# Finishing each expert's rows in the expert loop instead of in a combine stage (one decoder layer, one core)

## The reference

```python
# xt: 512 x 1024; 4 groups of 8 experts; each token picks 1 group and 2 experts in it
weights = g_w[:, None] * softmax(top_v)              # two weights per token
expert  = g_idx[:, None] * EXPERTS_PER_GROUP + top_i # two experts per token
h = silu(xb @ w_e_gate[e]) * (xb @ w_e_up[e])        # 1024 -> 512, twice
y = h @ w_e_down[e]                                  # 512 -> 1024
moe = sum of the token's two y rows, each times its weight
out = LayerNorm(ALPHA * x2 + moe)                    # ln2_g, ln2_b
```

## Time and profile before

| | us |
|---|---|
| median of 3 runs (lowest, highest) | 1359.92 (1359.82, 1360.22) |
| the profiled execution | 1359.31 |
| its span, first to last instruction | 1357.6 |
| TensorE busy in the span | 1235.4 (91%) |
| VectorE busy | 509.0 (37%) |
| ScalarE busy | 411.0 (30%) |
| GpSimd busy | 118.6 (9%) |
| mean granted TensorE clock | 0.969 |

### The profile page before, as it was taken

The page is one execution under the profiler, slowest core; times in us unless marked ns, Lnnn a source line. Parts: engine busy times, 40 slices in busy tenths (PEclk is TensorE's granted clock), DMA queues, the critical chain, the costliest instruction groups (busy, mean ns, idle before and its releaser), DMA issues.

```text
span 1357.6 us, 16490 instructions
## 1 busy us (share of the span) xinstructions
PE 1235.4 (91%) x5912; PEld 837.5 (62%) x5912; DVE 509.0 (37%) x780; ACT 411.0 (30%) x572; POOL 118.6 (9%) x168
## 2 busy tenths in 40 slices
PE   7999999999999999999998967999998888888860
PEld 6888878878888888888887863444433333333320
DVE  5487655336473473474348342000000000000008
ACT  5767673222432432432434021111111111111111
POOL 0000000000000000000051000211111111111112
PEclk9999999999999999999999976999999999999995
DMA  7232322353223133233233868999999999999954
GB/s 238 80 111 58 87 70 82 118 150 95 76 78 109 62 93 93 62 97 89 64 107 121 314 250 318 400 404 406 406 404 407 409 407 408 397 406 397 404 224 167
DMA packets 202069, 294.15 MB, mean 217 GB/s; under 512 B 11678, under 2 KB 109070, under 8 KB 201520
## 3 DMA queue, kind: packets, MB, share of 16 engines
q1 hardware_dynamic: 195568, 281.00, 57.7%
q0 software_dynamic: 5312, 8.47, 1.7%
q10 hardware_dynamic: 1152, 4.19, 0.8%
HBM read 289.89 MB, written 12.65 MB: 223 GB/s over the span
## 4 chain that ended last, share of the span: by engine, by line
PE 71%; DMA 19%; DVE 4%; SPq 3%; issue 2%; ACT 1%; POOLq 0%; ACTq 0%; POOL 0%; DVEq 0%
PE bank L1384 18%; PE bank L1385 18%; PE bank L1386 18%; DMA m_raw<-in_w_e_down_dram 9%; DMA m_raw<-in_w_e_up_dram 9%; PE bank L1624 8%; PE bank L1646 4%; SPq L388 2%; PE bank L1634 2%; PE bank L1558 1%; PE bank L1607 1%; DVE x L1372 1%; DVE wo_lo L881 1%; PE bank L1486 1%; DMA xg<-x_dram,first_x 0%
## 5 line engine op out<-in xcount | busy, mean ns | idle before, releaser
L1624 PE MATMUL bank<-m_raw,xe 128*64 128x512 f32 x1024 | 243.3, 610 | 34.4 <-DMA m_raw<-in_w_e_up_dram 29.3
L1384 PE MATMUL bank<-xt_hi,w_hi 128*128 128x512 f32 x576 | 225.0, 391 | 2.2 <-ACT merge L684 1.0
L1386 PE MATMUL bank<-xt_hi,w_lo 128*128 128x512 f32 x576 | 224.2, 389 | 0.0
L1385 PE MATMUL bank<-xt_lo,w_hi 128*128 128x512 f32 x576 | 224.1, 389 | 0.0
L881 DVE TENSOR_TENSOR w_lo<-raw,w_hi 128x1024 fp32r<-128x1024 f32 x120 | 148.4, 1238 | 184.7 <-ACT w_hi L595 183.3
L1624 PEld LDWEIGHTS bank<-m_raw,xe 128*64 128x64 f32 x1024 | 67.8, 138 | 184.0 <-issue 118.6
L595 ACT ACTIVATE w_hi<-raw 128x1024 fp32r<-128x1024 f32 x120 | 126.1, 1056 | 172.2 <-PE bank L1386 172.1
L1646 PE MATMUL bank<-m_raw,ht 128*64 128x512 f32 x512 | 121.3, 601 | 10.3 <-DMA m_raw<-in_w_e_down_dram 8.7
L1384 PEld LDWEIGHTS bank<-xt_hi,w_hi 128*128 128x128 f32 x576 | 108.1, 188 | 25.6 <-ACT merge L684 1.4
L1386 PEld LDWEIGHTS bank<-xt_hi,w_lo 128*128 128x128 f32 x576 | 108.1, 188 | 22.3
L1385 PEld LDWEIGHTS bank<-xt_lo,w_hi 128*128 128x128 f32 x576 | 108.2, 188 | 22.2
(11 more groups left out here) (237 smaller groups left out, 1630.7 us busy)
## 6 DMA issues: line engine op xcount, KB each, us to landing
m_raw<-in_w_e_gate_dram SPq DMA_DIRECT2D x64, 1024.0 KB, 16.0
m_raw<-in_w_e_up_dram SPq DMA_DIRECT2D x64, 1024.0 KB, 14.9
m_raw<-in_w_e_down_dram SPq DMA_DIRECT2D x64, 1024.0 KB, 14.0
raw<-in_w_in_dram SPq DMA_DIRECT2D x88, 512.0 KB, 4.0
raw<-in_w_ret_o_dram SPq DMA_DIRECT2D x16, 512.0 KB, 3.4
raw<-in_w_lru_o_dram SPq DMA_DIRECT2D x16, 384.0 KB, 3.0
raw<-in_w_out_dram SPq DMA_DIRECT2D x8, 512.0 KB, 3.5
y_rows<-y_dram SPq DMA_DIRECT2D x4, 1024.0 KB, 7.9
```

Of the source, the lines that this page charges most:

```text
L1384: pe.matmul(dst, sh, mh, start=first and x == 0, stop=False)
L1385: pe.matmul(dst, sh, ml, start=False, stop=False)
L1386: ins = pe.matmul(dst, sl, mh, start=False, stop=last and x == n - 1)
L1624: last = pe.matmul(bank[side:side + ROWS, b, :], xe[:, 4 * half + k, :], m_raw[v.slot][:, FE * k:FE * k + FE], start=half == 0 and k < 2, ...
```

## The change

- Rows are handled in halves of 512 columns: partitions 0 to 63 hold the left half of up to 64 rows, 64 to 127 the right half. `xg` becomes three buffers of 128x512, `turn_x` four 128x128 transposes.
- A token's pick with the lower expert number is its first, the other its last. `y_out` multiplies by the pick's weight. The first pick's row is scattered to `y_dram` (zeroed early in the kernel, so that it holds zeros where nothing came first); the last pick's expert gathers it (`y_first`), adds ALPHA times x2 (`base`) and its own y (`total_row`), takes statistics, lets TensorE join the two halves' means and variances (`moments`), normalises (`finish`) and scatters the rows to the output.
- The combine stage and the scaling of x2 by ALPHA on ScalarE go.
- The ring has 21 buffers, filled by a list ORDER, in which the last expert's gate comes before and its up after the down of expert 30; nine units instead of seven are loaded before the projection is done.
- The experts are written out instead of looped.
- The router also builds lists of the picks that are first and last and of their weights (32 more small matmuls and about 15 small VectorE operations).

```diff
-MRING = 18
+ORDER = [(part, 0, half) for part in "gu" for half in range(2)]
+for _e in range(EXPERTS - 2):
+    ORDER += [(part, _e + (part != "d"), half) for part in "gud" for half in range(2)]
+ORDER += [(part, _e, half) for part, _e in (("g", EXPERTS - 1), ("d", EXPERTS - 2), ("u", EXPERTS - 1), ("d", EXPERTS - 1)) for half in range(2)]
+AT = {what: n for n, what in enumerate(ORDER)}
+M_END = len(ORDER)
+MRING = 21
...
+            def load_m(slot, consumed, part, e, half):
+                sp.wait_ge(m_done, consumed)
+                w, k, n = {"g": (w_gate, 4, FE), "u": (w_up, 4, FE), "d": (w_down, 2, D)}[part]
+                src = w[:, e, k * half:k * half + k, :] if isinstance(e, int) else w[:, ds(e, 1), k * half:k * half + k, :].rearrange("p e k n -> p (e k) n")
+                sp.dma_start(m_raw[slot][:, :].rearrange("p (k n) -> p k n", k=k), src).then_inc(m_loaded[slot], 16)
+
+            def load_units(a, b):
+                for n in range(a, b):
+                    load_m(n % MRING, n + 1, *ORDER[n])
+
+            load_units(0, 9)
             sp.wait_ge(proj_ok, TT)
+            load_units(9, 16)
+            for side_h in range(2):
+                for x, name in enumerate(("ln2_g", "ln2_b")):
+                    sp.dma_start(ln2[ROWS * side_h:ROWS * side_h + ROWS, x, :],
+                                 io[name][0:1, HALF * side_h:HALF * side_h + HALF].rearrange("a n -> (a n)").partition_broadcast(ROWS)).then_inc(ln2_in, 16)
             sp.wait_ge(x2_ok, TT)
+            load_units(16, 17)
             sp.wait_ge(routed, TT)
+            load_units(17, 18)
+            sp.wait_ge(x2_stored, 16 * TT)
+            sp.wait_ge(x2_turned, TT)
+            load_units(18, 20)
+            sp.wait_ge(picks_ok, 1)
+            load_units(20, M_END)
...
+            pool.memset(zeros[:, :], 0.0).then_inc(list_set, 1)
+            pool.wait_ge(list_set, 3)
+            pool.wait_ge(conv_ok, 3)
+            pool.dma_start(y_dram.rearrange("(n p) d -> p n d", p=P), zeros[:, :].unsqueeze(1).to_broadcast([P, 2 * TOKENS // P, HALF])).then_inc(y_empty, 16)
...
-            def rows_next(e, first_turn=None):
-                pool.wait_ge(xe_turned, e + 3)
-                pool.sem_inc(marks, 1)
-                gather(e + 3, first_x)
-                if first_turn is None:
-                    free_y(e - 1)
-                else:
-                    with pool.If(first_turn > 0):
-                        free_y(e - 1)
-                send(e, e, first_y)
-
-            with pool.Fori(0, TURNS) as i:
-                steps.enter(i, 2 * BODY)
-                for b in range(BODY):
-                    rows_next(BODY * i + b, None if b else i)
-                steps.leave(TURNS)
-            rows_next(EXPERTS - 2)
-            free_y(EXPERTS - 2)
-            send(EXPERTS - 1, EXPERTS - 1, first_y)
-            free_y(EXPERTS - 1)
+            for e in range(3):
+                rows_in(xg[:, e, :], x2_halves, col(all_x, e), xg_in[e])
+            pool.wait_ge(picks_read, 3)
+            for e in range(EXPERTS):
+                if 3 <= e + 2 < EXPERTS and e > 0:
+                    pool.wait_ge(z0_ok, e)
+                    pool.wait_ge(xe_turned, e)
+                    rows_in(xg[:, (e + 2) % 3, :], x2_halves, col(all_x, e + 2), xg_in[(e + 2) % 3])
+                pool.wait_ge(y_ok, e + 1)
+                rows_out(y_dram, y_sb[:, :], col(all_first, e), y_sent)
+                if e + 1 < EXPERTS:
+                    pool.wait_ge(z0_ok, e + 1)
+                    pool.wait_ge(y_sent, 16 * e + 16)
+                    rows_in(y_first[:, :], y_dram, col(all_last, e + 1), y_first_in)
+                pool.wait_ge(f_ok, e + 1)
+                rows_out(out_halves, z[:, e % 2, :], col(all_last, e), stored[e % 2])
...
+            def y_out(s, consumed, w):
+                act.wait_ge(m_done, consumed)
+                if not (isinstance(s, int) and s == 0):
+                    act.wait_ge(y_sent, 16 * s)
+                    act.wait_ge(z_done, s + (isinstance(s, int) and s == EXPERTS - 1))
+                act.activation(y_sb[:, :], bank[:, 2, :], ACT.Identity, scale=w).then_inc(y_ok, 1)
+
+            def root(s):
+                act.wait_ge(f_var, s + 1)
+                act.activation(std[:, :], lnv[:, 3:4], ACT.Sqrt, bias=eps[:, :]).then_inc(f_std, 1)
...
+            act.wait_ge(ovf_ready, 1)
+            gate_evict(used("g", 0))
             xe_out(1)
             silu_part(0)
+            act.wait_ge(picks_read, 3)
+            for e in range(EXPERTS - 1):
+                gate_evict(used("g", e + 1))
+                if e:
+                    root(e - 1)
+                if e + 2 < EXPERTS:
+                    xe_out(e + 2)
+                y_out(e, used("d", e), all_w[:, e:e + 1])
                 silu_part(e + 1)
+            root(EXPERTS - 2)
+            y_out(EXPERTS - 1, used("d", EXPERTS - 1), all_w[:, EXPERTS - 1:EXPERTS])
+            root(EXPERTS - 1)
...
+            def h_part(s, hb):
                 dve.wait_ge(m_silu, s + 1)
+                tt(ht[:, hb, :, :], bank_t[:, 1, :, :], silu[:, :, :], ALU.mult).then_inc(ht_ok, 1)
+            def base(s, xb, zb, landed, free):
+                dve.wait_ge(xg_in[xb], landed)
+                if not (isinstance(s, int) and s == 0):
+                    dve.wait_ge(y_first_in, 16 * s)
+                if not (isinstance(s, int) and s < 2):
+                    dve.wait_ge(stored[zb], free)
+                dve.scalar_tensor_tensor(z[:, zb, :], xg[:, xb, :], ALPHA, y_first[:, :], ALU.mult, ALU.add).then_inc(z0_ok, 1)
+            def total_row(s, zb):
+                dve.wait_ge(z0_ok, s + 1)
+                if isinstance(s, int) and s == EXPERTS - 1:
+                    dve.wait_ge(m_done, used("d", s))
+                    dve.scalar_tensor_tensor(z[:, zb, :], bank[:, 2, :], all_w[:, s:s + 1], z[:, zb, :], ALU.mult, ALU.add).then_inc(z_done, 1)
+                else:
+                    dve.wait_ge(y_ok, s + 1)
+                    tt(z[:, zb, :], z[:, zb, :], y_sb[:, :], ALU.add).then_inc(z_done, 1)
+                dve.wait_ge(z_done, s + 1)
+                step(dve.bn_stats(stats[:, 0:6], z[:, zb, :]))
+                step.wait()
+                dve.sem_inc(marks, 1)
+                dve.bn_aggr(pairs[:, :], stats[:, 0:6]).then_inc(pairs_ok, 1)
+            def finish(s, zb):
+                zt = z[:, zb, :]
+                dve.wait_ge(paired, s + 1)
+                step(dve.tensor_copy(lnv[:, 0:3], bank[:, 6, 0:3]))
+                step.wait()
+                dve.scalar_tensor_tensor(lnv[:, 3:4], lnv[:, 2:3], lnv[:, 2:3], lnv[:, 1:2], ALU.mult, ALU.add).then_inc(f_var, 1)
+                step(dve.scalar_tensor_tensor(zt, zt, lnv[:, 0:1], ln2[:, 0, :], ALU.subtract, ALU.mult))
+                dve.wait_ge(f_std, s + 1)
+                step(dve.reciprocal(rstd[:, :], std[:, :]))
+                step.wait()
+                dve.scalar_tensor_tensor(zt, zt, rstd[:, :], ln2[:, 1, :], ALU.mult, ALU.add).then_inc(f_ok, 1)
+            def used(part, e):
+                return AT[part, e, 1] + 1 + MRING
+            up_evict(used("u", 0))
+            h_part(0, 0)
+            dve.wait_ge(picks_read, 3)
+            dve.wait_ge(ln2_in, 64)
+            for e in range(EXPERTS - 1):
+                late = e == EXPERTS - 2
+                if not late:
+                    up_evict(used("u", e + 1))
+                if e:
+                    finish(e - 1, (e - 1) % 2)
+                base(e, e % 3, e % 2, 16 * (e // 3 + 1), 16 * (e // 2))
+                total_row(e, e % 2)
+                if late:
+                    up_evict(used("u", e + 1))
+                h_part(e + 1, (e + 1) % 2)
+            e = EXPERTS - 1
+            finish(e - 1, (e - 1) % 2)
+            base(e, e % 3, e % 2, 16 * (e // 3 + 1), 16 * (e // 2))
+            total_row(e, e % 2)
+            finish(e, e % 2)
...
+            def turn_x(s, xb, landed):
+                pe.wait_ge(xg_in[xb], landed)
                 if not (isinstance(s, int) and s == 0):
                     pe.wait_ge(xe_ok, s)
                 pe.sem_inc(marks, 1)
+                for j in range(KD // 2):
+                    last = pe.transpose(bank_x[:, j, :], xg[:, xb, P * j:P * j + P], ident[:, :])
                 last.then_inc(xe_turned, 1)
...
+            def moments(s):
+                pe.wait_ge(pairs_ok, s + 1)
+                if not (isinstance(s, int) and s == 0):
+                    pe.wait_ge(f_var, s)
+                pe.matmul(bank[:, 6, 0:2], mean_of[:, :], pairs[:, :], start=True, stop=True)
+                pe.matmul(bank[:, 6, 2:3], diff_of[:, :], pairs[:, 0:1], start=True, stop=True).then_inc(paired, 1)
+            turn_x(0, 0, 16)
+            gate_up(0, 0)
+            turn_x(1, 1, 16)
             pe.wait_ge(ovf_ok, 1)
             pe.transpose(bank[0:1, 7, 256:256 + P], ovf_col[:, :], ident[:, :]).then_inc(ovf_turned, 1)
-            pe.wait_ge(fold_ok, 2)
```

(74 more changed lines are left out.)

385 lines of the change are left out of this document (160 added, 225 removed).

## The result

The change makes the kernel slower by a fifth: 1628.3 us (1624.2 to 1632.2, four runs) against 1359.9; the ratio is 1.198, with a 95% interval of 1.196 to 1.201. The forecast was 1620, range 1525 to 1715. The profiled execution took 1632.2 for a span of 1630.4. Of the runs behind this page, two of the kernel before and one each of the two experiments with eight dummies and with 18 ring buffers fell into a slower state, and all medians leave them out.

The account below looks back on a forecast made before the run. The prediction took the weight stream to bound the kernel before, and a serial gather the changed one: 856.5 + 29 x 25.3 + 28 = 1618 us of span, plus 2.3, gives 1620 us; range 1525 to 1715.

Parts of the forecast that it names:

- The main step: GpSimd's queue: gather of rows e+2 waits behind finish(e-1) and the output scatter, in series with TensorE; stall 9.3 us per expert.
- GpSimd: wake, scatter, gap: Between finish and gather: 0.79 from releasing event, 1.04 scatter, 0.8 before the second indirect DMA; sum 2.6 us.
- gather, issue to landing: Indirect DMA of rows e+2 into xg: 4.0 us, between 2.4 alone and 6.0 under a saturated weight stream.
- clock: TensorE after each stall: granted clock falls, costing 3.0 us extra per expert, ends 0 and 3.6.
- period: One expert of the serial loop: 13.0 work, 9.3 stall and 3.0 clock make 25.3 us, against the stream's 15.6.
- it runs dry near the time at which the gather's data start: Weight stream refilling six units: 15.6 us of transfers; the gather's data start 15.2 us after down.
- Rival (a): Gather meets a still backed-up weight stream and takes 6.0 us; period 27.3, time 1678; chance 0.20.
- The fit of the Trainium skill: GpSimd DMA as 2.0 us plus bytes over 436 GB/s: 2.3 us per mean gather, final figure about 50 us lower.
- Start and tail: Before the serial loop: 2.0 us later start, gate/up at 856.5; after fold(30): 28 us to the end.
- What was set down as hidden: Work off the critical path, costing nothing: table loads, y chain (14.3 us after a down), zero fill, h_part.
- Rival (b): TensorE's clock stays up or falls only briefly in the stall; period 22.3, time about 1531; chance 0.20.
- (c): Expert loop: chain fits under the weight stream, period 15.6 us, tail gains 35; time 1324; chance 0.05.

Follow-up runs that it names:

- eight dummies: Changed kernel with eight unused float32 matmuls on TensorE between moments and the transposes, inside the stall; 1594.0 us.
- 18 ring buffers: The kernel with the gather issued ahead of the f_ok wait, its ring cut from 21 to 18 weight buffers; 1328.9 us, ratio 0.979.
- half the traffic: Changed kernel with every weight load after the first 21 cut to its first half, instructions and waits kept; 1574.6 us, ratio 1.160.
- ten dummies: Changed kernel with ten unused matmuls on TensorE between moments and the transposes, inside the stall; 1569.7 us.
- e1_early: Changed kernel with only the gather moved: rows e+3 requested right after the scatter of y(e), no longer behind f_ok; 1322.0 us, ratio 0.974.
- e1_again: e1_early run once more unchanged, beside the run with two dummies for the last expert; 1319.9 us, ratio 0.974.

## Why the prediction was right

The main step, that the order of GpSimd's queue puts the gather of rows e+2 in series with TensorE in 29 iterations, is shown by the chain of waits and by the run that moves only that issue (1628 to 1322). It was found by following one iteration through the queues in program order, at a place where the trace of before shows no wait.

Term by term, forecast against measured:

| term, us per expert | forecast | measured |
|---|---|---|
| up eviction with wake | 0.74 | 0.71 |
| finish | 1.9 | 1.86 |
| GpSimd: wake, scatter, gap | 0.79 + 1.04 + 0.8 | 0.83 + 1.01 + 0.30 |
| gather, issue to landing | 4.0 | 5.34 |
| wake of TensorE | 0.1 | 0.14 |
| clock | 3.0 | 2.25 |
| gate, up, down, fold, transposes at full clock | 13.0 | 13.1 |
| period | 25.3 | 25.67 |

The measured terms add up to 25.55; of the missing 0.12, 0.09 is a single period in which the output scatter started 2.5 us late.

Three terms were off and nearly cancelled: over 29 periods the gather was taken 39 us too low, the gap and the clock together 36 us too high. That the mechanism was right is no luck; that the time came within 8 us is.

- The gap between two indirect DMAs is 0.30, so of the 0.8 seen before each issue 0.5 belongs to the wake.
- The gather took 5.3, near the loaded rows. The step that was off is "it runs dry near the time at which the gather's data start". The first of the six units was issued at 1109.4, 2.2 us before that down ended, as forecast, but the refill took 20 us at 330 GB/s where the prediction had 15.6 at 404. It ran dry near 1129, 17.5 us after the down and not 13.6, and the gather's data, which were to start at 1126.3, met three microseconds of it. Rival (a), the loaded gather, was nearer in this term, though not in the sum. Why the stream is slower while it refills than under saturation was not tested.
- The clock's price was taken at 3.0 and is 2.25 in the mean; with half the traffic it is 2.8 (5.9 for down).

The fit of the Trainium skill, "DMA: Bandwidth & Descriptors", anatomy of one DMA, gave an estimate of 2.3 us for such a gather. It agrees within 0.6 with the half-traffic run's 2.8 to 2.9 and not with the loaded 5.3. Naming it as a lower figure was fair; used for the sum it would have made the forecast 50 us lower, 1570.

Start and tail: the first gate and up of the serial iterations began at 855.8 (forecast 856.5). From the end of the last fold but one, 1601.5, to the end of the span are 28.9 us (forecast 28). Here too two errors cancel: the last down ran at full clock (3.68), so the 3 us set down for it were not needed, while the last scatter took 4.4 us from its start to the end of the span (forecast 2.4), and small waits of the statistics and the moments took the rest.

What was set down as hidden stayed hidden: the table loads (the one for the square root ran from 1117.7 to 1119.0, before gate and up ended at 1120.5), the y rows, the zero fill, h_part. VectorE's waits for y_first, 93 us in all, delayed nobody on the chain. The y chain's slack was small, though: in the profile of the ten dummies, y_first's gather is once issued so late (1098.84) that the output scatter starts right behind it, 0.4 us later than in the other periods.

Rival (b) fell with the clock rows; even with the clock held by ten dummies the time is 1570 and not its 1531. (c), 1324, is what the kernel gives once the order is mended, 1322. Of its gain of 35 us, the tail can be read directly: 10.7 us from the last down's end (1309.7) to the end of the span (1320.4), where it was 42.6. Three ring slots gave 7, and 2.1 MB more of output in the stream take about 5 back (worked out at 404 GB/s, not isolated).

## What to carry to other kernels

Queues run in order, so each wait added ahead of an early request delays that request too. Before adding a step to an engine that also issues prefetches, write down one iteration in program order and ask what the prefetch now stands behind; another buffer does not help if the issue itself waits. Price a pause of TensorE with the slow clock after it, and a small DMA by what shares its queues at that moment.

## What the hardware showed beyond that

- A gather of up to 128 half rows takes 2.8 to 2.9 us from issue to landing beside half the weight traffic and 5.3 to 6 beside a weight stream; starting it 1.3 us earlier changed that by only 0.3 (5.33 to 5.65).
- Back to back, indirect DMAs of GpSimd are 0.30 us apart; after a wait for VectorE the next one starts 0.83 after VectorE's end.
- Pauses of 2.2 to 3.4 us (8 dummies) lost the clock in 13 of 28 periods, and not the longer ones rather than the shorter; pauses of 0.6 to 1.9 us (10 dummies) lost it in none of 28. At the end of e1_early a row of pauses of about 1 us did lose it, and the same row in e1_again did not. What decides it is open.
- The pause was shorter with half the traffic and yet down longer (5.9 against 5.4 us); the cause is open.
